# Convolution layer of a two-block kernel: seventh stacked quad for the last tile, products of ones around the norm's sums, and the next layer's first two tiles taken feature by feature

## The reference

```python
def conformer_conv(h, w_pw1, b_pw1, w_dw, b_dw, ln_g, ln_b, w_pw2, b_pw2):
    u = h @ w_pw1 + b_pw1
    a, gate = jnp.split(u, 2, axis=-1)
    u = a * jax.nn.sigmoid(gate)
    u = causal_dwconv_2(u, w_dw, b_dw)
    u = jax.nn.silu(layernorm(u, ln_g, ln_b))
    return u @ w_pw2 + b_pw2
```

## Time and profile before

| | |
|---|---|
| median of three runs | 1078.83 us (1078.76 to 1080.79) |
| profiled execution, its own time | 1081.06 us |
| its span, first to last instruction | 1079.3 us |
| TensorE busy | 1045.7 us (97%) |
| weight loads busy | 989.6 us (92%) |
| DVE busy | 756.6 us (70%) |
| ACT busy | 525.8 us (49%) |
| POOL busy | 147.1 us (14%) |
| mean granted TensorE clock | 0.989 of 2.4 GHz |

### The profile page before, as it was taken

One profiled execution on the slowest core, in us unless ns is written; L12 is line 12 of the kernel. 1 busy time (PEld: TensorE's weight loads), 2 busy tenths in 40 slices (PEclk: granted clock), 3 DMA queues, 4 the chain that ended last, 5 costly groups with the idle time before them and its releaser, 6 DMA issues. The chain is left out here.

```text
span 1079.3 us, 22383 instructions
## 1 busy us (share of the span) xinstructions
PE 1045.7 (97%) x8495; PEld 989.6 (92%) x8495; DVE 756.6 (70%) x1211; ACT 525.8 (49%) x900; POOL 147.1 (14%) x198
## 2 busy tenths in 40 slices
PE   9999889799999999998999999999998999999998
PEld 8999669699999999876999999999986699999998
DVE  6876767576666666784877777777967667767776
ACT  6443555554444446325644444465745555444442
POOL 0070020011222110002001000030114600010000
PEclk9998999999999999998999999999999999999999
DMA  9553305256556664650565555556640036655551
GB/s 354 160 186 87 98 20 179 75 163 191 176 192 194 193 180 124 205 172 8 171 210 183 189 180 191 193 146 167 237 134 22 1 120 181 206 180 191 177 194 58
DMA packets 51043, 169.73 MB, mean 157 GB/s; under 512 B 5664, under 2 KB 10784, under 8 KB 50848
## 3 DMA queue, kind: packets, MB, share of 16 engines
q1 hardware_dynamic: 45216, 163.22, 47.0%
q10 hardware_dynamic: 5760, 5.57, 2.0%
HBM read 162.15 MB, written 1.05 MB: 151 GB/s over the span
## 5 line engine op out<-in xcount | busy, mean ns | idle before, releaser
L1493 DVE TENSOR_TENSOR WL<-WR,WH 128x1024 fp32r<-128x1024 f32 x302 | 373.1, 1252 | 140.7 <-ACT WH L1240 138.4
L854 PE MATMUL acc<-XH,WH 128*128 128x256 f32 x1392 | 401.5, 288 | 2.5 <-DVE XP L1510 1.7
L856 PE MATMUL acc<-XH,WL 128*128 128x256 f32 x1392 | 393.4, 283 | 0.0
L855 PE MATMUL acc<-XL,WH 128*128 128x256 f32 x1392 | 393.0, 282 | 0.0
L1240 ACT ACTIVATE WH<-WR 128x1024 fp32r<-128x1024 f32 x302 | 312.2, 1050 | 117.2 <-PE acc L856 81.7
L854 PEld LDWEIGHTS acc<-XH,WH 128*128 128x128 f32 x1392 | 266.0, 191 | 6.2 <-DVE WL L1493 3.5
L855 PEld LDWEIGHTS acc<-XL,WH 128*128 128x128 f32 x1392 | 266.1, 191 | 0.8
L856 PEld LDWEIGHTS acc<-XH,WL 128*128 128x128 f32 x1392 | 266.1, 191 | 0.0
L854 PE MATMUL big<-UH,WH 128*128 128x256 f32 x608 | 168.7, 277 | 0.3 <-POOL UL L1974 0.3
L855 PE MATMUL big<-UL,WH 128*128 128x256 f32 x608 | 168.3, 277 | 0.0
L856 PE MATMUL big<-UH,WL 128*128 128x256 f32 x608 | 168.0, 276 | 0.0
(11 more groups left out here) (290 smaller groups left out, 1280.9 us busy)
## 6 DMA issues: line engine op xcount, KB each, us to landing
WR<-weights SPq DMA_DIRECT2D x302, 512.0 KB, 3.7
STK<-UP ACTq DMA_DIRECT2D x32, 138.0 KB, 3.5
X<-x_t SPq DMA_DIRECT2D x4, 256.0 KB, 6.1
MEM<-mem_t SPq DMA_DIRECT2D x1, 1024.0 KB, 9.7
result_t<-X SPq DMA_DIRECT2D x4, 256.0 KB, 2.2
CON<-constants SPq DMA_DIRECT2D x1, 880.0 KB, 12.4
CBUF<-KCV ACTq DMA_DIRECT2D x4, 128.0 KB, 5.8
CBUF<-KCV ACTq DMA_DIRECT2D x4, 127.5 KB, 7.1
```

The lines of the kernel that those rows point to most:

```text
L854: pe.matmul(out, wh, hi, start=start, stop=False, skip_group_check=True)
L855: pe.matmul(out, wh, lo, start=False, stop=False, skip_group_check=True)
L856: return pe.matmul(out, wl, hi, start=False, stop=stop, skip_group_check=True)
L1493: dve.tensor_tensor(WL[:, cs % SPL], WR[:, cs % RAW], WH[:, cs % SPL].bitcast(F32), ALU.subtract).then_inc(w_low, 1)
```

## The change

It does three things. (a) The last convolution tile, j = 7, gets a seventh quad: taps 24 to 27 move from DVE to TensorE, four more matmuls, and DVE keeps three taps of that tile. A new array `DGL` holds its diagonals, made by POOL in one instruction at j = 24 of the first feed-forward; all rows of `STK` grow from 276 to 280 elements. (b) Of the 18 idle passes, 6 stand ahead of `sum_squares("ln")` and 16 behind it. (c) ACT does only the Silu, DVE makes the high part `YH`, and the first two tiles of pw2 are made together, feature by feature.

```diff
-STACKED = T + 4 * (QUADS - 1)
+STACKED = T + 4 * QUADS
...
+("w_last", 4),
...
+("DGL", [P, 4, 32], F32)
...
-                for m in range(QUADS):
+                quads = QUADS + int(j == KD - 1)
+                if j == KD - 1:
+                    pe.wait_ge(sem("diagonals"), 2 * KD + 1)
+                for m in range(quads):
                     for g in range(4):
-                        ins = pe.matmul(big[32 * g:32 * g + 32, j % 4, 0:T], DG[:, j, g * QUADS + m, :],
-                                        STK[:, j % UPS, g, 4 * m:4 * m + T], start=m == 0, stop=m == QUADS - 1,
-                                        skip_group_check=True)
+                        w = DG[:, j, g * QUADS + m, :] if m < QUADS else DGL[:, g, :]
+                        ins = pe.matmul(big[32 * g:32 * g + 32, j % 4, 0:T], w, STK[:, j % UPS, g, 4 * m:4 * m + T],
+                                        start=m == 0, stop=m == quads - 1, skip_group_check=True)
...
             sum_features(KD - 1).then_inc(sem("mean_ps"), 1)
+            acc_ready(TILE["pw2"])
+            acc_ready(TILE["pw2"] + 1)
+            idle_passes(TILE["pw2"], 6)
             sum_squares("ln")
-            acc_ready(TILE["pw2"])
-            idle_passes(TILE["pw2"], 18)
-            for j in range(KD):
-                tile(START["pw2"] + j, TILE["pw2"] + j, YH, YL, base=(yl_ready, Y_BASE["pw2"]) if j == 0 else None)
+            idle_passes(TILE["pw2"], 16)
+            for j in range(2):
+                chunk_ready(START["pw2"] + j)
+            for k in range(KD):
+                pe.wait_ge(yl_ready, Y_BASE["pw2"] + k + 1)
+                for j in range(2):
+                    c, t = START["pw2"] + j, TILE["pw2"] + j
+                    ins = three(acc[:, t % 2, 0:T], c % SPL, k * P, YH[:, k], YL[:, k], k == 0, k == KD - 1)
+                    if k == KD - 1:
+                        ins.then_inc(w_used, 1)
+            for j in range(2, KD):
+                tile(START["pw2"] + j, TILE["pw2"] + j, YH, YL)
...
                 act.wait_ge(gy_ready, GY_BASE["pw2"] + k + 1)
-                silu = ch.add(act.activation(GY[:, k], GY[:, k], ACT.Silu, bias=vec("ln_b", k), scale=vec("ln_g", k)))
-                if k >= 1:
-                    act.wait_ge(act_chain, silu - 1)
-                    act.activation(YH[:, k - 1], GY[:, k - 1], ACT.Copy).then_inc(yh_ready, 1)
-            act.wait_ge(act_chain, silu)
-            act.activation(YH[:, KD - 1], GY[:, KD - 1], ACT.Copy).then_inc(yh_ready, 1)
+                act.activation(GY[:, k], GY[:, k], ACT.Silu, bias=vec("ln_b", k),
+                               scale=vec("ln_g", k)).then_inc(sem("normed"), 1)
...
-                    if n == 0:
+                    if n == (4 if j == KD - 1 else 0):
...
-                    own_taps(j, 0, OWN)
+                    own_taps(j, 4 if j == KD - 1 else 0, OWN)
...
+            def normed_high(k):
+                dve.wait_ge(sem("normed"), k + 1)
+                dve.tensor_copy(YH[:, k], GY[:, k]).then_inc(yh_ready, 1)
+
             for k in range(KD):
                 dve.tensor_tensor(GY[:, k], CX[:, k], RS2[:, :], ALU.mult).then_inc(gy_ready, 1)
+                if k >= 4:
+                    normed_high(k - 4)
+            for k in range(KD - 4, KD):
+                normed_high(k)
...
+            def last_diagonals():
+                pool.tensor_tensor(DGL[:, :, :], con("ident4").unsqueeze(1).broadcast_to([P, 4, 32]),
+                                   VEC[:, VCOL["w_last"]:VCOL["w_last"] + 4].unsqueeze(2).broadcast_to([P, 4, 32]),
+                                   ALU.mult).then_inc(sem("diagonals"), 1)
...
+                if j == 24:
+                    last_diagonals()
```

More of the change, by code:

```diff
@@ L53 @@
            ("mem_g", 8), ("ff_g", 8), ("final_g", 8), ("mix2_g", 16), ("ffn2_g", 16), ("b_pw1", 16),
-           ("w_dw", 8 * 4 * QUADS), ("w_own", 8 * OWN), ("b_dw", 8), ("ln_g", 8), ("ln_b", 8), ("b_pw2", 8),
+           ("w_dw", 8 * 4 * QUADS), ("w_last", 4), ("w_own", 8 * OWN), ("b_dw", 8), ("ln_g", 8), ("ln_b", 8), ("b_pw2", 8),
            ("q_g", 1), ("kc_g", 1), ("ks_g", 1), ("kw_g", 1), ("fconv", 2 * UP_TILES * 4),
@@ L171, in program @@
                    ("CX", [P, KD, T], F32), ("MU", [P, T], F32), ("CD", [P, 2, T], F32), ("STK", [P, UPS, 4, STACKED], F32),
-                   ("DG", [P, KD, 4 * QUADS, 32], F32)])
-        SG, AT, UPAD, CX, MU, CD, STK, DG = (B[n] for n in ("SG", "AT", "UP", "CX", "MU", "CD", "STK", "DG"))
+                   ("DG", [P, KD, 4 * QUADS, 32], F32), ("DGL", [P, 4, 32], F32)])
+        SG, AT, UPAD, CX, MU, CD, STK, DG, DGL = (B[n] for n in ("SG", "AT", "UP", "CX", "MU", "CD", "STK", "DG", "DGL"))
         C = group([("GU", [P, 2, T], F32), ("UH", [P, 2, T], F32R), ("UL", [P, 2, T], F32R),
@@ L2104, in stacked @@
     def stacked(w):
-        w = w[:4 * QUADS].reshape(QUADS, 4, 8, 4, 32)
+        w = w.reshape(-1, 4, w.shape[1] // P, 4, 32)
         return w.transpose(4, 1, 2, 3, 0).reshape(P, -1)
@@ L2122 @@
         "b_pw1": _features(a["conv_b_pw1_2"][0][gate_then_a], 16),
-        "w_dw": stacked(a["conv_w_dw_2"][0]), "w_own": taps(a["conv_w_dw_2"][0][4 * QUADS:], 8), "b_dw": _features(a["conv_b_dw_2"][0], 8),
+        "w_dw": stacked(a["conv_w_dw_2"][0][:4 * QUADS]),
+        "w_last": stacked(a["conv_w_dw_2"][0][4 * QUADS:4 * QUADS + 4, 7 * P:]), "w_own": taps(a["conv_w_dw_2"][0][4 * QUADS:], 8), "b_dw": _features(a["conv_b_dw_2"][0], 8),
         "ln_g": _features(a["conv_ln_g_2"][0], 8), "ln_b": _features(a["conv_ln_b_2"][0], 8),
```

## The result

The changed kernel takes 1083.38 us in the median of seven runs (1082.25 to 1086.55); the kernel before, run on the same chip, 1080.05 (1078.76 to 1082.13). The ratio is 1.0033, 95% interval 1.0019 to 1.0046: 3.3 us slower. The prediction was 1073.4, faster, with 1076.2 as its upper bound. The profiled execution after is the slowest of its seven, 1086.55 us, with a span of 1084.8 against 1079.3 before.

A forecast was written before the change was run, and what follows sets the result against it. TensorE, busy 97% of the span, bounds the kernel, so the end moves only where it idles or runs at its lower clock. 1.67 + 2.72 - 0.4 + 1.4 = 5.4 us off the 1078.83 median gives 1073.4, range 1071.8 to 1076.2.

The forecast's parts named there:

- Step 1: Convolution's last tile: with the seventh quad the last sum of features starts 1.67 us earlier; wider STK and extra diagonals cost nothing.
- Step 2: Ahead of the squares: six idle passes take 1.3 us, end at 488.6 before the first square at 488.95, delaying nothing.
- Step 3: Squares at the convolution's end: the clock holds once the gaps of 1.87 and 1.42 us go, gaining 2.72 us.
- Step 4: Silu to eighth YL, high copies on DVE: 8.1 us against 7.70, losing 0.4, between +0.65 and -1.3.
- rival A: The forecast case, DVE copies exclude POOL's YL: gain 4.4 to 5.7 us, 1073.1 to 1074.4, chance 0.53.
- B: Silu to eighth YL: copies do not hold POOL up, eighth YL at 7.05, 1072.5 to 1071.9 us, chance 0.28.
- Step 5: First two pw2 tiles made together: about 1.4 us saved net of a new 1.1 us stall; ffn0 at 522.2.
- ffn0's first evacuation: Start of ffn0: released at 528.3, wanted at 528.4, so it just fits; 0.0 to 0.3 us may be lost.
- D: The clock falls within pw2, costing 1.8 us: 1075.2 us, chance 0.06.
- C: The clock still falls ahead of the squares, losing 2.7 us: 1076.1 us, chance 0.07.
- E: Slower: the DVE and POOL port stretches each YL to 1802 ns, 1080.7 to 1081 us, chance 0.03.
- F: No change: the clock losses at squares and pw2 and slow bound of Step 4 together cancel 5.4 us, chance 0.03.

The follow-up runs named there:

- e1: Kernel before plus an unused 32-byte array behind VEC, moving every later array by 32 bytes: 1088.52 us, ratio 1.008.
- e13: Kernel before with 32 unused bytes ahead of UH, moving only UH, UL and five arrays behind them: 1088.38 us, ratio 1.0075.
- e2: Whole change, new diagonals taken from four unused columns of w_own so VEC keeps its size: 1076.43 us, ratio 0.9954 to the kernel before.
- e18: Changed kernel with 224 unused bytes ahead of UH, so UH lies 256 bytes later than before: 1075.35 us, ratio 0.9941 to the kernel before.
- e9: Kernel before plus seventh quad and six and sixteen idle passes, without the address shift; single run, ffn0 at 39.29 us in the stage against 43.16 before.
- e10: Whole change without the address shift, high copies left on ACT; single run, ffn0 at 37.32 us in the stage against 43.16 before.
- e8: Kernel before plus the seventh quad alone, without the address shift; single run, ffn0 at 38.78 us in the stage against 43.16 before.
- e3: Kernel before with 64 unused bytes ahead of WR, moving the weights and everything behind them: 1067.38 us, ratio 0.9883.
- e6: Kernel before with 32 unused bytes ahead of WR, moving the weights and everything behind them: 1075.47 us, ratio 0.9962.
- e7: Kernel before with 128 unused bytes ahead of WR, moving the weights and everything behind them: 1079.45 us, ratio 0.9994.
- e12: e5 with the first pw2 tile's bank released as soon as it has been read: 1061.6 us, ratio 0.9818 to the kernel before.
- e5: Changed kernel with VEC kept at its size and 64 unused bytes ahead of WR: 1063.66 us, ratio 0.9835 to the kernel before.

## Why the prediction was wrong, point by point

**Step 1** failed in one sentence: "Both count nothing", of the edits that come with the seventh quad. It weighed the wider `STK` rows and POOL's diagonals and left out the four columns of `VEC`, which stood in the diff as `("w_last", 4)`. They issue nothing and nobody waits for them, but they move `UH`: 7.6 us, more than all gains together. The term that the sum lacks is that one. e1 and e13 show this as a cause by itself, e2 and e18 show the change without it. No rival had it, not even the one that ended on the slower side. The rest of the step held: the add at 1.74 for 1.62, the first square at 4.52 for 4.50. In e18, where the taps waited for their transfer, the square stood at 5.39, so the 1.67 is 0.8 to 2.1 from execution to execution.

**Step 2** held: the six idle passes end ahead of the first square, and of the kernels that have them e9 shows the first square at 4.93, e10 and e2 at 4.32 and 4.09, against 4.46 in e8 without them: no cost that stands out of the scatter.

**Step 3** was right for the profiled pair (6.39 to 3.76, 2.63 for the forecast 2.72) and mis-sized for the kernel: it took the fall of one execution for a fixed cost. Over ten executions it is 1.0 us. It also read the fall as one "after these", after both gaps. The earlier trace rows has it between 489.0 and 489.5, and the second gap runs to 490.62: so in that execution only the first gap and most of the last sum lay ahead of it. This takes 1.7 off the sum for medians, 5.4 to 3.7; e2 gained 5.0 with an interval of 3.0 to 7.0 (ratio 0.9935 to 0.9972 of 1080.6), which does not decide between them.

**Step 4** held: 7.89 for 8.1, within 7.05 and 9.0. A copy on DVE waits for a POOL operation that is running. The row shows it: the first cast takes 0.29 us alone, the second, at 502.44, 0.82; it ends 0.16 behind the `YL` that was running until 503.10. The `YL` are 1.07 apart (502.26, 503.33), later 0.73 (3.66 for five), where I had 1.12 and 0.75. POOL alone had 0.68, so what a copy takes from POOL in its turn is 0.05 at most. That is rival A's mechanism, and not B's, which had put the eighth `YL` at 7.05. Against ACT's copies the move to DVE costs 0.22 us (e10 against e2). By the rule of the Trainium skill that the prediction named (SBUF — State Buffer, "SBUF: two separate sides"), a copy in a two-port mode would be locked out like this; the trace agrees for DVE's side, and does not show in what mode the copy ran.

**Step 5** held: 1.36 (e10 against e9) for 1.4, a stall of 0.91 for 1.1, ffn0 at 37.73 for 37.75, and neither ffn0's first evacuation nor a clock fall in pw2 (D) took anything back; the granted clock was 1.00 from 486 to 530. C did not come either. E and F, the rivals of no gain, looked for it in the port and the clock, and neither is where it went.

So the sum for the profiled pair is: -5.4 in the stage, +7.6 in the wide products, and +3 that lies ahead of the stage and is of that execution (0.8 for the first weights and 0.2 up to 184 us, 1.2 for the lower clock behind it, 0.8 at the first stacked copies), together +5.2 of the span's 5.5. Where the last 0.3 comes from is open. For the medians, -4.2 (e2) and +7.9 (e1) make +3.7, and 3.3 was measured.

The same section of the Trainium skill says that on the engines' side only the port pair shared by VectorE and GpSimd causes contention, and that TensorE never waits on another engine. Here the same 24 passes take 2.74 or 2.84 us by where their operand lies, which this sentence gives no reason for. No run here shows whether TensorE waits for another engine in them; what they lose the time to is open.

**What stays open.** Why, with the rest in its old place, `UH` is faster at a distance of 192 than at 64 or 224, and what the slower paces of `XH` at 0, 128 and 224 have to do with it; whether `WH` or another array read at the same time is the partner, since e3, e6 and e7 move all arrays behind `YH` together; why the layout with all operands at 192 runs at 2.72 in e3 and e12 near 300 us but at about 2.83 in e3's last two feed-forwards, in e12's pw2 and in e12's last feed-forward, and at 2.82 near 300 us in the profiled run of e5, whose other runs were up to 14 us faster; and why e7 alternates. More than one mechanism may be at work. What makes the clock fall in one execution and not in another with the same gaps is open too. That 32 bytes of `UH` cost the 7.6 us, and 256 give them back, does not rest on any of these.

## What to carry to other kernels

When an edit adds columns or an array, compare the offsets of all later arrays before and after, and read the mean of groups that the edit does not touch: 4 ns on each of 1824 passes outweighed a stage's gain of 5.4 us. Keep the sizes (here four unused columns did it), or pad to the same distance modulo 256 bytes, and try a few distances between moving operand and weights: one gap of 64 bytes was worth more than twice the whole change. Time each layout several times: one of them lay between 1059 and 1073 us. A clock fall seen in one profiled execution is a chance, not a cost; look at it in several before you price its removal.

## What the runs showed of the hardware that was not expected

- Passes of 256 columns at the full clock lie 0.114 us apart over `UH` at distance 192 from the weights and 0.118 at 224 (2.74 and 2.84 over 24), and 0.119 over `XH` at 0 (2.86). With all operands at 192 they lie 0.113 or 0.118 apart, by execution and by layer (2.72 or 2.83). Moving everything together changes nothing (ratio 0.9993); moving `UH` by 32 bytes costs 0.75%, by 256 nothing (0.9998).
- The same code lost the clock in some executions only. With a first gap of 1.87 us or more it fell in four of four, with 0.77 to 1.67 us in one of six. It fell ahead of the second gap in two of the five and behind it in three, and squares to Ln took 6.4 or 5.4 us accordingly, 3.76 where it held.
- A DVE cast from SBUF to SBUF with one input waits while POOL's subtraction runs: it takes 0.82 us for 0.29.
